# Two-layer hybrid mixer: block 1 normed inside the first projection of each latent pass, and the last output products finished tile by tile

## What is computed

```python
hx = _rmsnorm(x, g_pre) * (1.0 + scale_x) + shift_x
px = _in_proj(hx, w_in, IN_NAMES)            # 62 tiles of 128 columns
# ... window attention with sink, short conv, retention, 2-D Fourier: ys, each gated by silu(z)
for i in range(N_BRANCH):
    total = total + gates[:, :, i] * ((ys[i] * jax.nn.silu(zs[i])) @ w_os[i])
y = total @ w_out
x_new = x + gate_x * _rmsnorm(y, g_post)
```

## Time and profile before

| | |
|---|---|
| median of 3 runs | 2622.7 us (2622.6 to 2623.03) |
| the profiled execution: its own time | 2627.45 us |
| its span in the trace | 2625.3 us |
| mean granted PE clock | 0.982 |

### The profile page before, as it was taken

One profiled execution on the slowest core, in us unless ns is written; L12 is line 12 of the kernel. 1 busy time (PEld: TensorE's weight loads), 2 busy tenths in 40 slices (PEclk: granted clock), 3 DMA queues, 4 the chain that ended last, 5 costly groups with the idle time before them and its releaser, 6 DMA issues.

```text
span 2625.3 us, 38817 instructions
## 1 busy us (share of the span) xinstructions
PE 2501.9 (95%) x12993; PEld 2097.0 (80%) x12993; DVE 1141.9 (43%) x1698; ACT 1113.4 (42%) x2321; POOL 1221.6 (47%) x992
## 2 busy tenths in 40 slices
PE   7888989999999999999999989999999999999997
PEld 1887978799888767787888778898888788888886
DVE  2443656396255333333343365691534423333332
ACT  2645553396222554434433433693214333343332
POOL 1666973123222378855555442122213455555553
PEclk9899999999999999999999989999999999999999
DMA  6345752100121255544433431001211333344333
GB/s 248 94 131 170 217 164 89 36 1 20 49 63 29 61 147 159 159 121 143 135 108 105 140 117 47 13 1 42 64 36 35 101 109 111 112 143 137 108 112 120
DMA packets 393273, 262.38 MB, mean 100 GB/s; under 512 B 16934, under 2 KB 365750, under 8 KB 391610
## 3 DMA queue, kind: packets, MB, share of 16 engines
q1 hardware_dynamic: 378944, 227.07, 29.4%
q10 hardware_dynamic: 14204, 33.67, 3.7%
HBM read 251.23 MB, written 9.45 MB: 99 GB/s over the span
## 4 chain that ended last, share of the span: by engine, by line
PE 82%; DVE 5%; POOL 5%; issue 4%; ACT 2%; DMA 1%; DVEq 0%; ACTq 0%; SPq 0%; POOLq 0%
PE ps L725 78%; POOL w_lo L623 3%; PE ps L884 2%; POOL w_lo L616 1%; DMA w_raw<-in_w_in 1%; DVE r_prev L2073 1%; DVE softmax_stats L1966 1%; DVE a_probT_lo L1707 0%; PE ps L757 0%; ACT w_hi L1219 0%; DMA w_ada<-in_w_ada 0%; PE ps L824 0%; DVE a_out_sum L1707 0%; DVE norm_tmp L1852 0%; PE ps L870 0%
## 5 line engine op out<-in xcount | busy, mean ns | idle before, releaser
L616 POOL TENSOR_TENSOR w_lo<-w_raw,w_hi 128x512 fp32r<-128x512 f32 x644 | 883.7, 1380 | 995.4 <-ACT w_hi L1219 989.1
L725 PE MATMUL ps<-hT_hi,w_hi 128*128 128x512 f32 (+1 forms) x2528 | 945.8, 374 | 44.6 <-POOL w_lo L623 15.1
L725 PE MATMUL ps<-hT_hi,w_lo 128*128 128x512 f32 (+1 forms) x2528 | 933.1, 369 | 0.0
L725 PE MATMUL ps<-hT_lo,w_hi 128*128 128x512 f32 (+1 forms) x2528 | 933.0, 369 | 0.0
L1219 ACT ACTIVATE w_hi<-w_raw 128x512 fp32r<-128x512 f32 x760 | 472.6, 629 | 970.9 <-PE ps L725 879.8
L725 PEld LDWEIGHTS ps<-hT_hi,w_hi 128*128 128x128 f32 x2528 | 483.1, 191 | 138.9 <-POOL w_lo L616 15.3
L725 PEld LDWEIGHTS ps<-hT_hi,w_lo 128*128 128x128 f32 x2528 | 483.0, 191 | 78.7
L725 PEld LDWEIGHTS ps<-hT_lo,w_hi 128*128 128x128 f32 x2528 | 483.5, 191 | 75.6
L1707 DVE TENSOR_TENSOR merge_tmp<-merge_tmp,ps 128x512 f32<-128x512 f32 (+1 forms) x160 | 101.4, 634 | 659.3 <-PE ps L725 409.7
L623 POOL TENSOR_TENSOR w_lo<-w_raw,w_hi 128x512 fp32r<-128x512 f32 x116 | 154.4, 1356 | 57.0 <-ACT w_hi L1219 56.5
L1707 DVE TENSOR_TENSOR merge_tmp<-merge_tmp 128x512 f32<-128x512 f32 (+1 forms) x120 | 165.1, 1376 | 4.1
(11 more groups left out here) (268 smaller groups left out, 3005.0 us busy)
## 6 DMA issues: line engine op xcount, KB each, us to landing
w_raw<-in_w_in SPq DMA_DIRECT2D x476, 256.0 KB, 2.9
w_raw<-in_w_o_rest SPq DMA_DIRECT2D x112, 256.0 KB, 2.8
w_raw<-in_w_out SPq DMA_DIRECT2D x74, 256.0 KB, 2.7
w_ada<-in_w_ada SPq DMA_DIRECT2D x8, 1536.0 KB, 9.3
w_raw<-in_w_ada SPq DMA_DIRECT2D x48, 256.0 KB, 2.8
w_raw_more<-in_w_in SPq DMA_DIRECT2D x72, 128.0 KB, 2.5
w_raw<-in_w_o_attn SPq DMA_DIRECT2D x32, 256.0 KB, 2.8
w_raw<-in_dft_x SPq DMA_DIRECT2D x16, 256.0 KB, 2.7
```

Of the source, the lines that this page charges most:

```text
L616: eng.tensor_tensor(w_lo[:, r, :], raw[:, r, :], w_hi[:, r, :].bitcast(F32), ALU.subtract).then_inc(sem["w_split"], tally.up("w_split"))
L725: return eng.matmul(dst, lhsT, rhs, start=start, stop=stop)
```

## The change

1. `first_tiles`: in both latent passes PE works the first two tiles (four units, all kept in the ring) for block 0 alone, with two turns of block 1 behind each unit, and then the four units for block 1. The context pass's output product has no turns any more.
2. `last_units`: in block 1 of a latent pass the last output half leaves its last units (two in layer 0, four in layer 1) for the end, and does them one token tile after the other. Each tile's square, root, gate, result and send follow it, in `out_tiles` of ACT and DVE.
3. ACT's splits move to fit: in the context pass all eight stand ahead of the wait for the totals; in layer 0's last product one of the four after `out_squares(0)` goes behind the sends. One unit more is split ahead at the start of a latent pass.
4. DVE scales block 1 of the first latent pass after the last total. Several buffers move, the two extra weight buffers (`raw_more`) onto the modulation's rows, so their first load waits for `mod_cols`. The stage ends between context pass, latent pass and late pass go for ACT and DVE.

```diff
+        def by_tiles(p, b):
+
+            if p.ctx or b < p.NB - 1:
+                return 0
+            return 4 if p.layer + 1 == DEPTH else 2
...
+                elif u < HEAD_RING and u >= RING:
+                    eng.wait_ge(sem["mod_cols"], 1)
...
-                low_parts(first + LOOK)
+                low_parts(first + LOOK + (0 if p.ctx else 1))
...
+            def first_tiles(p):
+
+                for name in () if p.kept else ("hT_low", "hT_low_odd"):
+                    eng.wait_ge(sem[name], tally.now(name))
+                slots = []
+                for n in range(4):
+                    t, u = n // 2, n % 2
+                    if u == 0:
+                        eng.wait_ge(sem["proj_out"], tally.take("proj_out"))
+                    slots.append(slot())
+                    for k in range(4):
+                        w = slice(k * P, (k + 1) * P)
+                        three(ps[:, 2 * t, 0:p.BW], w_hi[:, slots[n], w], w_lo[:, slots[n], w], hT[0][:, 4 * u + k, 0:p.BW],
+                              hT[1][:, 4 * u + k, 0:p.BW], u == 0 and k == 0, u == 1 and k == 3)
+                    if n == 0:
+                        eng.wait_ge(sem["y_out"], tally.now("y_out"))
+                    if n == 1 and p.kept:
+                        eng.wait_ge(sem["raw_free"], 2 + raw_no[p.n - 1, R_V + 1] + 1)
+                    for k in (2 * n, 2 * n + 1):
+                        turn_tokens(p, 1, k, turn_bank(k))
+                for n in range(4):
+                    t, u = n // 2, n % 2
+                    if t == 0:
+                        for name in ("hT_low", "hT_low_odd"):
+                            eng.wait_ge(sem[name], tally.now(name, 2 * u + 2))
...
+                def last_units():
+
+                    rs, count = [], by_tiles(p, b)
+                    for t in range(p.TB):
+                        for n in range(count):
+                            if t == 0:
+                                rs.append(slot())
+                            w, k = slice(t * P, (t + 1) * P), KT - count + n
+                            last = three(ps[:, out_bank(p, 1, t), :], tot[0][:, k, w], tot[1][:, k, w],
+                                         w_hi[:, rs[n], :], w_lo[:, rs[n], :], False, n == count - 1)
+                            if t + 1 == p.TB:
+                                last.then_inc(sem["w_used"], tally.up("w_used"))
+                            elif n == count - 1:
+                                last.then_inc(sem["out_tile"], tally.up("out_tile"))
...
-                        if p.opens and (half == 0 and k >= 4 or half == 1 and k < 4):
-                            kk = k - 4 + 8 * half
-                            turn_tokens(early, 1, kk, kk % 4)
...
-                project(p, 6, True)
-                if p.done == p.NB:
-                    eng.wait_ge(sem["y_out"], tally.now("y_out"))
+                if p.ctx:
+                    norm(p)
+                    pe_goes_on(eng, tally)
+                    eng.wait_ge(sem["hT_pre"], tally.now("hT_pre", 4))
+                    project(p, 6, True)
+                else:
+                    pe_goes_on(eng, tally)
+                    first_tiles(p)
+                    project(p, 4)
...
-                split_high(2 if latent else 8)
+                split_high(2 if on else 8)
...
+                def out_tiles():
+
+                    eng.wait_ge(sem["out_mean"], tally.take("out_mean"))
+                    act(stat[:, 2, 0:p.TB], stat[:, 1, 4:4 + p.TB], ACT.Sqrt).then_inc(sem["act_own"], tally.up("act_own"))
+                    eng.wait_ge(sem["act_own"], tally.now("act_own"))
+                    for t in range(p.TB):
...
+                        act((sq_junk_late if on else sq_junk)[:, :], ps[:, out_bank(p, 1, t), :], ACT.Square,
+                            accum_out=stat[:, 0, 4 + t:5 + t]).then_inc(sem["y_out"], tally.up("y_out"))
+                        eng.wait_ge(sem["y_out"], tally.now("y_out"))
+                        act(stat[:, 2, t:t + 1], stat[:, 0, 4 + t:5 + t], ACT.Sqrt, scale=1.0 / D,
+                            bias=stat[:, 1, 4 + t:5 + t]).then_inc(sem["out_root"], tally.up("out_root"))
+                        if t:
+                            send_tile(p, b, t - 1)
+                    send_tile(p, b, p.TB - 1)
+                    tally.skip("y_gate", p.TB)
                 split_high(3)
                 out_squares(0)
-                split_high(4)
+                split_high(3 if on else 4)
+                if by_tiles(p, b):
+                    out_tiles()
+                    split_high(1)
+                    return
                 out_squares(1)
...
+                    for t in range(p.TB):
+                        if t + 1 < p.TB:
+                            eng.wait_ge(sem["out_tile"], tally.take("out_tile"))
+                        else:
+                            eng.wait_ge(sem["w_used"], tally.take("w_used__done", KT))
+                        eng.wait_ge(sem["y_out"], tally.take("y_out"))
+                        gated(1, t)
+                        eng.wait_ge(sem["out_root"], tally.take("out_root"))
+                        eng.reciprocal(stat[:, 1, t:t + 1], stat[:, 2, t:t + 1]).then_inc(sem["dve_own"], tally.up("dve_own"))
```

More of the change, by code:

```diff
@@ L177, in trunk @@
         W = RAW + 6144
[L178 removed]
+        raw_more = [at(f"w_raw_more{n}", [P, 2, 512], W + 1024 * n)[:, :, 256:512] for n in range(HEAD_RING - RING)]
         C = W + 18440
@@ L689, in norm @@
             def norm(p):
-                if p.late or p.done == p.NB:
+                if p.late:
                     tally.skip("hT_high", 2 * KT)
                     return
+                if not p.ctx and not p.kept:
+                    tally.skip("hT_high", KT)
                 for b in range(p.done, p.NB):
@@ L1119, in merge @@
                             eng.wait_ge(sem["hT_pre"], tally.now("hT_pre", 4))
[L1120 to L1123, removed]
-                        if p.opens and (half == 0 and k >= 4 or half == 1 and k < 4):
-                            kk = k - 4 + 8 * half
-                            turn_tokens(early, 1, kk, kk % 4)
+                    for k in range(KT - half * by_tiles(p, b)):
                         if half == 0 and k in (4, 6) and leads_on(p, b):
@@ L1312, in norm @@
             def norm(p):
-                for b in range(p.done, p.NB):
-                    for k in range(KT):
-                        high(p, b, k)
-                        if b + 1 < p.NB and k % 2:
-                            square(p, p.TB + k // 2)
-                    if b + 1 < p.NB:
-                        root(p, 1)
+                for k in range(KT):
+                    high(p, p.done, k)
             def evacuate(p, t, dst, func=ACT.Copy, **kw):
-                split_high(2)
+                split_high(2 - early_split[0])
+                early_split[0] = 0
                 if p.full and A_Q < t <= A_K:
@@ L1530, in merge @@
                 ada, on, latent = feeds_next(p, b), leads_on(p, b), normed_early(p, b)
-                if latent:
-                    behind, part = (latent, 1) if p.opens else (passes[p.n + 1], 0)
+                if on:
+                    behind, part = passes[p.n + 1], 0
                 def rows_and_tables():
@@ L1616, in merge @@
                     gated_high(p, b + 1)
-                if latent:
-                    if on:
-                        square(behind, 0)
-                        square(behind, 1)
+                if on:
+                    square(behind, 0)
+                    square(behind, 1)
                     split_high(1)
-                    if on:
-                        root(behind, part)
+                    root(behind, part)
                     split_high(1)
@@ L2266, in merge @@
                     if p.opens:
-                        for t in range(2, 4):
+                        for t in range(latent.TB):
                             scale_tile(latent, latent.TB + t)
@@ L2270, in merge @@
                         scaled(behind, part)
-                    for k in range(KT):
-                        shift(behind, part, k, k % 4)
-                        if k:
-                            low_part(behind, part, k - 1)
-                    low_part(behind, part, KT - 1)
+                        for k in range(KT):
+                            shift(behind, part, k, k % 4)
+                            if k:
+                                low_part(behind, part, k - 1)
+                        low_part(behind, part, KT - 1)
                 else:
```

88 lines of the change are left out of this document (60 added, 28 removed).

## The result

| | before | after |
|---|---|---|
| first measurement, median of 6 runs each | 2622.98 us | 2597.88 us (2591.24 to 2608.16) |
| its ratio | | 0.990, 95% interval 0.9878 to 0.9922 |
| second measurement, median | 2620.85 us (17 runs) | 2598.08 us (6 runs) |
| its ratio | | 0.9907, 0.9889 to 0.9925 |
| all runs of this study, median | 2621.48 us (43 runs) | 2597.88 us (12 runs) |

The change saves 23.6 us by all runs, where the prediction had 21.7. The forecast of 2601.0 us was 3.1 too high. The first ratio, put on the given 2622.7, makes 2596.5, half a microsecond under the low end of the range; the second makes 2598.3.

A forecast was written before the change was run, and what follows sets the result against it. PE, busy 95% of the span, was taken as the bound, with time to win only at its waits, low clock and tail. Savings 10.4 + 0 + 4.9 + 6.4 = 21.7 from 2622.7 gave 2601.0 us, range 2597 to 2609.

The forecast's parts named there:

- A: First boundary, context pass to first latent pass: turns leave the output product for the projection; saving 10.4 us.
- the cover of 1.6: First latent pass: VectorE's query tiles end at 449.6, PE asks for the value tile at 451.2; 1.6 us spare.
- B: Last product of latent pass 0, last two units tile by tile: saving 0, bounds -3 and +3 us.
- The walk through ScalarE's queue: Late pass: third unit's split behind all four sends, PE stands 5.3 us instead of 2.73, scaled tiles end unchanged.
- C: Second boundary, into the second latent pass: PE no longer waits for block 1; saving 4.9 us, bounds 3 and 6.
- a slow start at the low clock: First two tiles of the second latent pass: charged 1.5 us, taken from the profile before the change.
- D: The end: last four units tile by tile, results following each tile; saving 6.4 us, bounds 5.5 and 7.3.
- At nothing: Extra weight buffers load only at 57 us, wanted at 66.7: no cost, or a microsecond or two if that fails.
- 1: First-boundary product and layer 0's results: the feed stays the bound, 1.6 us a unit; 2608.4 us, chance 0.14.
- 2: Late pass: ScalarE's new order costs nothing, root 3 us earlier, first-boundary product at 1.37 a unit; 2596.7 us, chance 0.09.
- 3: Two mixed phases: interleaved turns hold PE at its lower clock, up to +43.8 us, 2644.8; chance 0.04.
- 4: First boundary: VectorE and the rope come late, 4 to 5 us beyond the cover; 2605.5 us, chance 0.13.

The follow-up runs named there:

- turns_first: Changed kernel with block 1's eight turns ahead of the first projected tiles in both latent passes, not between them: 2608.07 us, ratio 0.9949.
- mid_split: Changed kernel with two late-pass weight splits put between ScalarE's squares of layer 0's last tiles: 2590.41 us, ratio 0.9878.
- second_only: Kernel before the change with only `first_tiles` for the second latent pass and the unit split ahead for it: 2617.05 us, ratio 0.9981.
- mid_off: Changed kernel with layer 0's product by tiles alone undone, the end still by tiles: 2601.45 us.
- both_better: Changed kernel with two late-pass splits between ScalarE's last squares of layer 0, and three units by tiles at the end, not four: 2592.56 us, ratio 0.9874.

## Why the prediction was right, and where it was not

**A, 10.4 predicted, 9.6 measured** (9.5 to 9.9 in the other traces with the same part). A unit took 1.48 us and not 1.45 (0.5), and block 1's second half began 0.73 late, where I had called it just hidden; the turns took slightly less than the 0.51 I gave each. The clock was 1.00. Rope: the first one started at 400.85, 47.2 behind the product's start (46.7 predicted), and PE's wait at the value tile was 1.2, the same as before, so the cover of 1.6 held. The run turns_first gives the mechanism: 8.8 of the 9.6 are the interleaving.

**B, 0 predicted, 1.0 measured in the late pass.** The walk through ScalarE's queue was right in kind: the split came at 1492.88, behind the last send, and PE stood 4.6 us (5.3 predicted). The mis-sized term is the results: I gave 2.25 us a tile, and they came 1.99 apart (starts at 1485.16, 1487.15, 1489.15 and 1491.14). So the split came 5.3 us behind the product's end and not 6.1, which is 0.8 of the 1.0. The root of the norm came 21.9 us behind the product's end, where it was 22.9 before and I had it unchanged. I had the cost and the gain cancel; they did so but for this 1 us. Mid_split shows that the cost was 4.0 us.

**C, 4.9 predicted, 5.9 measured.** From the late pass's last turn to the end of the first two tiles it was 33.0 before and is 27.1. I charged 1.5 us for "a slow start at the low clock". There was none in either trace of the changed kernel: 26.4 us at 1.00. Where the low clock is there, the first two tiles take 28.0 (second_only), 28.1 (mid_off) or 28.9 (mid_split), and the saving is the 4.4 of second_only. The charge was right for some executions and wrong for others.

**D, 6.4 predicted, 6.7 measured.** The wait for the sixteenth low part was 0.63, but the product took 0.96 longer (0.8 predicted). The path behind the last matmul was 2.9 (3.1), and store and closing 3.2 (3.5), so PE's end to the span's end was 6.1, where the prediction named 6.6 to 7.

**At nothing:** PE's list of waits from 350 to 462 us shows no wait for the extra weight buffers, and at 60 to 70 us none that the kernel before didn't have.

**The step that failed.** The mechanism of all four parts stood; the sum was too small, 21.7 for the 23.2 that the traces show. The terms that were mis-sized are in B and C, 4.9 together for 6.9: the "slow start at the low clock" in C, taken at 1.5 us and measured at 0, and the results in B, taken at 2.25 us a tile and measured at 1.99. A took 0.8 of this back, and D added 0.3. The first of the two was carried over from one trace of the kernel before as if it were a property of the program. By the traces it is not: the same instructions ran with it in one trace and without it in another.

That explains 1.5 of the 4.5 us between the forecast of 2601.0 and the 2596.5 of the first ratio. The other 3.0 lie in no edited place. I put the low end at 2597 with rivals in mind but not the scatter that goes with the granted clock; the three runs given (2622.6 to 2623.03) didn't show it, and the 43 reach from 2618.3 to 2631.11. With 12 runs of the changed kernel at 2591 to 2608, on which side of 2597 the first ratio falls is chance for the greater part; the second ratio falls on the other side.

**Rivals.** *1* (the feed stays the bound, 2608.4) is out: the product took 1.48 us a unit and not 1.6, and the only wait for a low part that is listed around it is under half a microsecond. *2* came nearest in number (2596.7) and is wrong in mechanism: ScalarE's order costs 4.0, the root of the norm came 1.0 earlier and not 3, and A was not at 1.37 a unit. *3* (the clock falls in the mixed phases through the turns, some 22 to 44 us) is out: it was 1.00 in both phases of the changed kernel, and turns alone held it for 35 us. Three other traces had a low clock at the start of the second mixed phase, for 1.6 to 2.5 us, in mid_split ahead of the first turn. The rule from the Trainium skill's page "TensorE: Matmul & The Clock Gate", Part 4: PE-mode transpose, on which it rested, does not hold for these turns where the clock is up when they begin. *4* is out: same wait at the value tile as before.

## What to carry to other kernels

Work for which PE must wait on other engines at each step pays between matmuls that don't need it: the same eight turns in a block cost 8.8 us more than interleaved, where 0.73 us of waiting was left. When results are moved tile by tile, look at what else stands in the queue of the engine that makes them: here two weight splits behind four sends hid a gain of 4 us, and moving them between the squares gave it back. Read a gain from several traces, cut at common events; two traces of one program differed by 4.5 us at the same event. A low clock read in one trace is no fixed cost of the stretch that it stands in: over the same tiles, the same instructions had none in one trace and 2.5 us of it in another.

## What was not expected of the hardware

The granted clock of one unchanged stretch (110 to 216 us) was 0.97 or 0.98 in some executions of a program and 0.87 or 0.89 in others, and the stretches behind it start some 5 us apart. The first two tiles of the second latent pass are the second such place (26.4 us at 1.00 in both_better, 28.9 at 0.91 in mid_split, in one program up to there, and out of the same wait). Over the 12 runs of the changed kernel, a clock of 0.994 went with 2591.24 us and one of 0.986 with 2608.16. What picks one or the other is open; no run here was made on it.

Turns of 128x128 in fp32 don't lower a clock that is up: 320 of them, 0.11 us each, twice at 1.00.
